# Last six steps of a seven-product down projection taken tile by tile, and the final LayerNorm of four tiles as two VectorE passes

## The chip, the core and the metric

The kernel runs on one core of one Trainium2 chip. The metric is device time in microseconds. Engines are named PE (TensorE matmul), PEld (TensorE weight load), DVE (VectorE), ACT (ScalarE), POOL (GpSimd) and SP (SyncE, which here only issues transfers).

## The reference, cut to what matters

The program is one inference step of a decoder layer for 1024 prompt tokens and 64 sample tokens, with 1024 model columns and an inner width of 2816. The part around the change is the second FFN and the last LayerNorm:

```
def layer_norm(x, g, b):
    xc = xf - mean(xf)
    return xc * rsqrt(mean(xc * xc) + LN_EPS) * g + b

def swiglu(x, wi, wo):
    g, u = split(x @ wi, 2)
    return (silu(g) * u) @ wo
...
x = layer_norm(ALPHA * x + 0.5 * swiglu(x, ffn_wi[0], ffn_wo[0]), ln_g[0], ln_b[0])
x = layer_norm(ALPHA * x + merged @ w_o, ln_g[1], ln_b[1])
x = layer_norm(ALPHA * x + 0.5 * swiglu(x, ffn_wi[1], ffn_wo[1]), ln_g[2], ln_b[2])
```

## The kernel before, in words

Every engine has its own program written out by hand, and engines wait for one another on counting semaphores. Nothing is scheduled by a planner in this part.

Both FFNs run the same code, `ffn(f)` with f = 0 and 1. The down product (`silu(g) * u` times `ffn_wo`) of the prompt is computed as seven block products, q = 0 to 6, instead of eight. Each product runs over KD = 11 blocks of the inner width, so there are STEPS = 77 steps t = 11q + k. One step brings a 128x512 block `h_raw` of activations and a 128x512 block of weights. Each f32 operand is split in two: ACT rounds it (`step_hi`: `h_hi`, `b_hi`, line L963 and L904), and DVE subtracts to get the rest (`step_lo`: `h_lo`, `b_lo`, L1397 and L1398, then `d_lo_ready`). PE then does four token tiles i = 0 to 3 of the step (`down_tile`), each with three matmuls of 512 columns (hi*hi, lo*hi, hi*lo; L2026 to L2028). Each tile i adds up in a PSUM bank of its own over the eleven steps. In the text "the lows of step t" are the two results of `step_lo` for step t.

Operands lie in three slots, t modulo 3. SP loads `h_raw` of step t once the lows of step t-3 are made; ACT writes slot t modulo 3 once PE has counted step t-3 as done (`step_done`). Between the lows of two steps DVE also does `step_extras`: it adds finished products into `y` and does the LayerNorm of tiles 0 to 3 and of the sample tile 8 (scale L1306, shift L1311, statistics L1550).

The last product, q = 6, is steps 66 to 76. PE takes steps 66 to 73 step by step. For the last three steps it waits for the lows of step 75, does steps 74 and 75 of tiles 0 and 1, waits for the lows of step 76, finishes tiles 0 and 1, and then does tile 2 and tile 3 whole. Tile i of this product becomes token tile 4+i of the output (columns 0 to 511; the other half was ready before).

After `ffn(1)` DVE adds each finished bank to `y` (L1285), takes the statistics of the half (L2006) and aggregates them (L2007). POOL makes the reciprocal root (`rstd`: add epsilon L730, power L731, minus mean times it L732). ACT normalises into two PSUM banks (L1238), DVE multiplies by the gain (L2011), and the shift by the bias is done on POOL for tiles 4 and 5 (L819, L821, L822) and on DVE for tiles 6 and 7 (L2014, L2016, L2017). SP stores tiles 0 to 3, 8, 4 and 5, ACT's queue stores tiles 6 and 7; tiles 5 and 7 go out in halves.

Of the kernel before, what the change touches and what calls it, by code (L numbers as in the profile page):

```python
# [277 lines left out]
def hybrid_layer(nc, w, c, o):  # L278
# [4 lines left out]
    with ExitStack() as ctx:  # L283
# [305 lines left out]
        def _(sp):  # L589
# [104 lines left out]
            store_y(8)  # L694
            store_y(4)
            wait_affine(sp, 2, 5)
            sp.dma_start(o["y_prompt"][0, 5 * P:6 * P, 0:512], y_half(5, 0)).then_inc(y_stored, 16)
            sp.wait_ge(ln_affine, affine_count(2, 5)[1] + 1)
            sp.dma_start(o["y_prompt"][0, 5 * P:6 * P, 512:D], y_half(5, 1)).then_inc(y_stored, 16)
            sp.wait_ge(y_stored, 16 * (NT + 2))  # L700
# [3 lines left out]
        def _(pool):  # L704
# [83 lines left out]
            def ffn(f):  # L788
# [26 lines left out]
                for t in range(4, 8):  # L815
                    rstd(k * NT + t + 1, t)
                if f:
                    pool.wait_ge(scaled_last, 1)
                    nc.gpsimd.tensor_tensor(y_tile(4), y_tile(4), ln_bd[:], ALU.add).then_inc(ln_affine, 1)  # L819
                    pool.wait_ge(scaled_last, 2)  # L820
                    nc.gpsimd.tensor_tensor(y_half(5, 0), y_half(5, 0), ln_bd[:, 0:512], ALU.add).then_inc(ln_affine, 1)  # L821
                    nc.gpsimd.tensor_tensor(y_half(5, 1), y_half(5, 1), ln_bd[:, 512:D], ALU.add).then_inc(ln_affine, 1)  # L822
# [1876 lines left out]
```

## Time and profile before

| | us |
|---|---|
| median of three runs | 2437.4 |
| lowest, highest | 2435.5, 2445.0 |
| span of the profiled execution (first to last instruction) | 2434.7 |
| DVE's last instruction ends | 2430.5 |
| PE's last matmul ends | 2421.7 |

The profiled execution has no device time of its own beside its span. The span lies 2.7 us under the median of the runs, and that difference is taken as what lies around it. All moments below are counted from the start of the span. In the profile of matmuls the start of one to the start of the next is the cost of one; the duration shown (0.39 us) includes a stretch that overlaps the next.

### The profile page before, as it was taken

The numbers are of one execution on the slowest core, as the hardware profiler recorded it, in microseconds if no ns is written. First come the engines' busy times: TensorE is split into PE (matmuls) and PEld (weight loads), VectorE is DVE, ScalarE is ACT, GpSimd is POOL, SyncE is SP. The second block draws the span as 40 slices with busy tenths as digits, with TensorE's granted clock in tenths as the row PEclk, the third lists the DMA queues.
The fourth block names the chain that finished last, engine by engine and source line by source line (L and its number), as shares of the span: only waits on it lengthen the run. The fifth ranks groups of instructions, "written<-read, shape, count | busy, mean of one in ns | idle before, by whom it ended". The sixth has DMA issues, their size and how long they took to land.

```text
span 2434.7 us, 31780 instructions
## 1 busy us (share of the span) xinstructions
PE 2395.3 (98%) x12613; PEld 2053.8 (84%) x12613; DVE 1660.1 (68%) x2305; ACT 910.8 (37%) x1325; POOL 205.3 (8%) x297
## 2 busy tenths in 40 slices
PE   8999999999999999999999999999999999999997
PEld 6888888888878898989999878888788888888786
DVE  6666565657787767666666867577866566665788
ACT  4222222243353336543347333373422222234344
POOL 3000000000021010000100111202300000000011
PEclk9999999999999999999999999999999999999999
DMA  4232222267444333243342445534222222327643
GB/s 144 87 125 82 89 89 95 83 218 232 131 140 142 110 111 111 96 127 90 114 126 87 140 141 169 169 96 148 74 97 81 96 100 91 104 96 225 200 147 129
DMA packets 225859, 300.08 MB, mean 123 GB/s; under 512 B 13424, under 2 KB 166304, under 8 KB 222880
## 3 DMA queue, kind: packets, MB, share of 16 engines
q1 hardware_dynamic: 211936, 240.43, 31.8%
q0 software_dynamic: 13056, 56.48, 6.3%
q8 instruction: 100, 1.64, 0.3%
q10 hardware_dynamic: 720, 1.15, 0.1%
q14 instruction: 47, 0.39, 0.0%
HBM read 243.81 MB, written 55.18 MB: 123 GB/s over the span
## 4 chain that ended last, share of the span: by engine, by line
PE 88%; DVE 6%; ACT 2%; DMA 2%; issue 1%; SPq 0%; POOL 0%; DVEq 0%; ACTq 0%
PE ps L2026 25%; PE ps L2027 25%; PE ps L2028 25%; PE ps L2123 2%; PE ps L2122 2%; PE ps L2202 1%; DVE xc_lo L1316 1%; PE ps L2203 1%; PE ps L2368 1%; DVE b_lo L1398 1%; DVE y L1285 1%; DVE w_lo L491 1%; PE ps L2503 1%; DMA raw<-in_w_in 1%; DVE h_lo L1397 1%
## 5 line engine op out<-in xcount | busy, mean ns | idle before, releaser
L2026 PE MATMUL ps<-xc_hi,u_hi 128*128 128x512 f32 x1232 | 482.7, 392 | 2.6 <-DVE u_lo L1357 1.5
L2027 PE MATMUL ps<-xc_lo,u_hi 128*128 128x512 f32 x1232 | 480.3, 390 | 0.0
L2028 PE MATMUL ps<-xc_hi,u_lo 128*128 128x512 f32 x1232 | 479.6, 389 | 0.0
L491 DVE TENSOR_TENSOR w_lo<-raw,w_hi 128x1024 fp32r<-128x1024 f32 x198 | 238.8, 1221 | 99.4 <-ACT w_hi L485 99.1
L2026 PEld LDWEIGHTS ps<-xc_hi,u_hi 128*128 128x128 f32 x1232 | 231.6, 188 | 49.2 <-DVE xc_lo L1316 1.7
L2028 PEld LDWEIGHTS ps<-xc_hi,u_lo 128*128 128x128 f32 x1232 | 231.2, 188 | 48.7
L2027 PEld LDWEIGHTS ps<-xc_lo,u_hi 128*128 128x128 f32 x1232 | 231.7, 188 | 44.7
L485 ACT ACTIVATE w_hi<-raw 128x1024 fp32r<-128x1024 f32 x198 | 205.5, 1054 | 161.4 <-PE ps L2028 95.6
L2026 PE MATMUL ps<-b_hi,h_hi 128*128 128x512 f32 x616 | 241.1, 391 | 1.7 <-DVE b_lo L1398 1.7
L2028 PE MATMUL ps<-b_hi,h_lo 128*128 128x512 f32 x616 | 239.8, 389 | 0.0
L2027 PE MATMUL ps<-b_lo,h_hi 128*128 128x512 f32 x616 | 239.7, 389 | 0.0
L2026 PE MATMUL ps<-w_hi,xg_hi 128*128 128x256 f32 (+1 forms) x640 | 219.2, 343 | 0.0
L2028 PE MATMUL ps<-w_hi,xg_lo 128*128 128x256 f32 (+1 forms) x640 | 215.1, 336 | 0.0
L2027 PE MATMUL ps<-w_lo,xg_hi 128*128 128x256 f32 (+1 forms) x640 | 215.0, 336 | 0.0
L963 ACT ACTIVATE h_hi<-h_raw 128x512 fp32r<-128x512 f32 x154 | 97.4, 632 | 271.2 <-PE ps L2028 175.5
L1357 DVE TENSOR_TENSOR u_lo<-wa,u_hi 128x1024 fp32r<-128x1024 f32 x88 | 108.8, 1236 | 107.3 <-ACT u_hi L904 107.3
L904 ACT ACTIVATE u_hi<-wa 128x1024 fp32r<-128x1024 f32 x88 | 93.0, 1057 | 203.6 <-PE ps L2123 109.9
L904 ACT ACTIVATE u_hi<-ws 128x1024 fp32r<-128x1024 f32 x66 | 70.0, 1060 | 241.9 <-PE ps L2028 148.3
L1397 DVE TENSOR_TENSOR h_lo<-h_raw,h_hi 128x512 fp32r<-128x512 f32 x154 | 106.0, 688 | 67.7 <-ACT b_hi L904 67.4
L2026 PEld LDWEIGHTS ps<-b_hi,h_hi 128*128 128x128 f32 x616 | 115.6, 188 | 30.1 <-issue 3.2
L2028 PEld LDWEIGHTS ps<-b_hi,h_lo 128*128 128x128 f32 x616 | 115.6, 188 | 24.4
L2027 PEld LDWEIGHTS ps<-b_lo,h_hi 128*128 128x128 f32 x616 | 115.6, 188 | 23.7
(330 smaller groups left out, 4572.9 us busy)
## 6 DMA issues: line engine op xcount, KB each, us to landing
raw<-in_w_in SPq DMA_DIRECT2D x90, 512.0 KB, 3.8
wa<-in_ffn_wi SPq DMA_DIRECT2D x88, 512.0 KB, 3.8
h_raw<-h_spill SPq DMA_DIRECT2D x154, 256.0 KB, 2.8
h_spill<-tm POOLq DMA_DIRECT2D x22, 1024.0 KB, 4.2
b_raw<-in_ffn_wo SPq DMA_DIRECT2D x66, 256.0 KB, 3.7
raw<-in_w_in SPq DMA_DIRECT2D x96, 128.0 KB, 2.5
raw<-in_w_in SPq DMA_DIRECT2D x48, 256.0 KB, 3.2
raw<-in_w_br_ret SPq DMA_DIRECT2D x24, 512.0 KB, 4.2
```

The source lines that it names most:

```text
L485: nc.scalar.activation(wslot(n, False), raw[:, s * D:(s + 1) * D], ACT.Copy).then_inc(hi_ready, 1)
L491: nc.vector.tensor_tensor(wslot(n, True), raw[:, s * D:(s + 1) * D], fr(wslot(n, False)), ALU.subtract).then_inc(lo_ready, 1)
L904: nc.scalar.activation(dst, src, ACT.Copy).then_inc(sem_, 1)
L963: nc.scalar.activation(h_hi[s][:], h_raw[s][:], ACT.Copy)
L1285: return nc.vector.scalar_tensor_tensor(out=out, in0=in0, scalar=scalar, in1=in1, op0=op0, op1=op1)
L1357: tt(u_lo[s][:], w_src[i][:], fr(u_hi[s][:]), ALU.subtract).then_inc(u_dve, 1)
L1397: tt(h_lo[s][:], h_raw[s][:], fr(h_hi[s][:]), ALU.subtract)
L2026: mm(out, a_hi, b_hi, start=first, stop=False)
L2027: mm(out, a_hi, b_lo, start=False, stop=False)
L2028: return mm(out, a_lo, b_hi, start=False, stop=last)
L2122: mm(out, lhs, u_hi[s][:, k * 2 * P:(k + 1) * 2 * P], start=first and k == 0, stop=False)
L2123: ins = mm(out, lhs, u_lo[s][:, k * 2 * P:(k + 1) * 2 * P], start=False, stop=last and k == 3)
```

## The change

For the second FFN alone, steps 71 to 73 write their split operands into three further slots (`end_...`), which lie where `t1` and the first column block of `t2` were, no longer read at that point. So steps 71 to 76 have six slots together. ACT no longer waits for PE before steps 71 to 73; for steps 74 to 76 it waits for step 68, 69, 70 to be done, as before in slot but without steps 71 to 73 between. `h_raw` keeps its three slots and its loads keep their waits. PE runs steps 0 to 70 as before and then takes steps 71 to 76 tile by tile: six steps of tile 0, where it waits in turn for the lows of each step, then six of tile 1, of tile 2 and of tile 3.

The first FFN has no further slots. Its last three steps are now also tile by tile from the first, with a wait for each step's lows, where before steps 74 and 75 of tiles 0 and 1 came ahead of the wait for step 76.

The final LayerNorm of tiles 4 to 7 is done by DVE alone but for the power: (y - mean) * gain in one pass and * rstd + bias in the next, both in `y`. DVE also adds epsilon, POOL does only the power, ACT does nothing but issue stores. DVE finishes a tile before it takes the next. Tile 7 is done in two halves. SP stores 8, 4 and 5 whole.

```
+        for j, tiles in enumerate((h_hi, h_lo, b_hi, b_lo)):
+            tiles += [at(f"end_{'hb'[j // 2]}{j % 2}_{i}", (149 + 2 * j + 8 * i) * K, 512, FR) for i in range(3)]
...
+        def slot_of_step(f, t):
+            return 3 + t - (STEPS - 6) if f and STEPS - 6 <= t < STEPS - 3 else t % 3
+        def steps_done_before(f, t):
+            return max(0, t - 5 if f and t >= STEPS - 3 else 0 if f and t >= STEPS - 6 else t - 2)
...
             def step_hi(f, t):
-                if t >= 3:
-                    act.wait_ge(step_done, STEPS * f + t - 2)
-                else:
+                if t < 3:
                     act.wait_ge(prod_done, product(f, UNITS - 1, 2))
+                elif steps_done_before(f, t):
+                    act.wait_ge(step_done, STEPS * f + steps_done_before(f, t))
...
-            for t in range(4, 8):
-                dve.wait_ge(ln_hat, hat_count(2, t))
-                dst = two_banks(LAST_BANK[t]) if t in DVE_AFFINE[2] else y_tile(t)
-                tt(dst, two_banks(LAST_BANK[t]), ln_gd[:], ALU.mult).then_inc(scaled_last, 1)
...
+                link(nc.vector.bn_aggr(mv[:, 2 * t:2 * t + 2], st6[:, 12 * t:12 * t + 12]))
+                nc.vector.tensor_scalar(ve[:, t:t + 1], mv[:, 2 * t + 1:2 * t + 2], LN_EPS, None, ALU.add).then_inc(ln_aggr, 1)
+                if t < 7:
+                    link(stt(y_tile(t), y_tile(t), mean, ln_gd[:], ALU.subtract, ALU.mult))
+                    dve.wait_ge(ln_rstd, hat_count(2, t))
+                    stt(y_tile(t), y_tile(t), rstd, ln_bd[:], ALU.mult, ALU.add).then_inc(ln_affine_v, 1)
+                    continue
+                for half in range(2):
+                    link(stt(yh, yh, mean, ln_gd[:, cols], ALU.subtract, ALU.mult))
+                    dve.wait_ge(ln_rstd, hat_count(2, t))
+                    stt(yh, yh, rstd, ln_bd[:, cols], ALU.mult, ALU.add).then_inc(ln_affine_v, 1)
...
-                last = STEPS - 3
-                pe.wait_ge(d_lo_ready, STEPS * f + last + 2)
-                for i in (0, 1):
-                    for t in (last, last + 1):
-                        down_tile(f, 6, i, t % KD, t % 3)
-                pe.wait_ge(d_lo_ready, STEPS * f + last + 3)
-                for i in (0, 1):
-                    down_tile(f, 6, i, KD - 1, (last + 2) % 3).then_inc(tile_done, 1)
+                for i in range(4):
+                    for t in range(first, STEPS):
+                        if i == 0:
+                            pe.wait_ge(d_lo_ready, STEPS * f + t + 1)
+                        ins = down_tile(f, 6, i, t % KD, slot_of_step(f, t))
```

(`first` is STEPS - 6 for the second FFN and STEPS - 3 for the first; `link` makes DVE wait for the instruction's own end.)

PE, end of the second FFN, before. Of each group of three matmuls the first stands here; `b_hi1,h_hi1` is step 73, `2` is step 74, `0` is step 75, then `1` step 76.

```order
L2026 MATMUL ps<-b_hi1,h_hi1 128x512 [waits d_lo_ready]
...
L2026 MATMUL ps<-b_hi1,h_hi1 128x512
...
L2026 MATMUL ps<-b_hi2,h_hi2 128x512 [waits d_lo_ready]
...
L2026 MATMUL ps<-b_hi0,h_hi0 128x512
...
L2026 MATMUL ps<-b_hi2,h_hi2 128x512
...
L2026 MATMUL ps<-b_hi0,h_hi0 128x512
...
L2026 MATMUL ps<-b_hi1,h_hi1 128x512 [waits d_lo_ready]
```

The same place in the change, from step 71 on (`end_b0_0` is the rounded weights of step 71, `end_b0_1` of 72, `end_b0_2` of 73):

```order
L2024 MATMUL ps<-end_b0_0,end_h0_0 128x512 [waits d_lo_ready]
...
L2024 MATMUL ps<-end_b0_1,end_h0_1 128x512 [waits d_lo_ready]
...
L2024 MATMUL ps<-end_b0_2,end_h0_2 128x512 [waits d_lo_ready]
...
L2024 MATMUL ps<-b_hi2,h_hi2 128x512 [waits d_lo_ready]
...
L2024 MATMUL ps<-b_hi0,h_hi0 128x512 [waits d_lo_ready]
...
L2024 MATMUL ps<-b_hi1,h_hi1 128x512 [waits d_lo_ready]
...
L2024 MATMUL ps<-end_b0_0,end_h0_0 128x512
```

Between two waits for lows there were twelve matmuls (four tiles) and are now three (one tile); 54 matmuls stand behind the last wait for tiles 1 to 3, where before there were 24 behind the wait for step 76.

DVE, the lows of steps 75 and 76 and what follows them, before:

```order
L1397 TENSOR_TENSOR h_lo0<-h_raw0,h_hi0 128x512 [waits d_hi_ready]
L1398 TENSOR_TENSOR b_lo0<-b21_t4,b_hi0 128x512
L1550 BN_STATS ln_stats<-y 128x6 [waits dve_step]
L1397 TENSOR_TENSOR h_lo1<-h_raw1,h_hi1 128x512 [waits d_hi_ready]
L1398 TENSOR_TENSOR b_lo1<-b21_t4,b_hi1 128x512
L1285 SCALAR_TENSOR_TENSOR y<-y,ps 128x512 [waits dve_step,tile_done]
L2006 BN_STATS ln_stats<-y 128x6 [waits tile_out]
L2007 BN_AGGR ln_mv<-ln_stats 128x2 [waits dve_step]
L1285 SCALAR_TENSOR_TENSOR y<-y,ps 128x512 [waits dve_step,tile_done]
```

The same place in the change:

```order
L1393 TENSOR_TENSOR h_lo0<-h_raw0,h_hi0 128x512 [waits d_hi_ready]
L1394 TENSOR_TENSOR b_lo0<-b21_t4,b_hi0 128x512
L1546 BN_STATS ln_stats<-y 128x6 [waits dve_step]
L1393 TENSOR_TENSOR h_lo1<-h_raw1,h_hi1 128x512 [waits d_hi_ready]
L1394 TENSOR_TENSOR b_lo1<-b21_t4,b_hi1 128x512
L1281 SCALAR_TENSOR_TENSOR y<-y,ps 128x512 [waits dve_step,tile_done]
L2002 BN_STATS ln_stats<-y 128x6 [waits tile_out]
L2003 BN_AGGR ln_mv<-ln_stats 128x2 [waits dve_step]
L2004 TENSOR_SCALAR ln_cols<-ln_mv 128x1 [waits dve_step]
L1281 SCALAR_TENSOR_TENSOR y<-y,ln_mv,ln_g_down 128x1024
L1281 SCALAR_TENSOR_TENSOR y<-y,ln_cols,ln_b_down 128x1024 [waits ln_rstd,dve_step]
L1281 SCALAR_TENSOR_TENSOR y<-y,ps 128x512 [waits dve_step,tile_done]
```

Up to the lows of step 76 nothing moved on DVE: the same instructions stand in the same order, those of steps 71 to 73 with other slots. Behind them each tile's two passes now stand ahead of the next tile's addition.

PE, end of the first FFN, before (`2` is step 74, `0` step 75, `1` step 76; the transposes of a tile of `y` stand in front):

```order
L2037 MATMUL ps<-ident,y 128x128 x7
L2026 MATMUL ps<-b_hi2,h_hi2 128x512 [waits d_lo_ready]
...
L2026 MATMUL ps<-b_hi0,h_hi0 128x512
...
L2026 MATMUL ps<-b_hi2,h_hi2 128x512
...
L2026 MATMUL ps<-b_hi0,h_hi0 128x512
...
L2026 MATMUL ps<-b_hi1,h_hi1 128x512 [waits d_lo_ready]
```

And in the change:

```order
L2035 MATMUL ps<-ident,y 128x128 x7
L2024 MATMUL ps<-b_hi2,h_hi2 128x512 [waits d_lo_ready]
...
L2024 MATMUL ps<-b_hi0,h_hi0 128x512 [waits d_lo_ready]
...
L2024 MATMUL ps<-b_hi1,h_hi1 128x512 [waits d_lo_ready]
...
L2024 MATMUL ps<-b_hi2,h_hi2 128x512
```

The wait for step 76 stood behind twelve matmuls and stands behind six.

## Rows read from the trace of the kernel before

**Rows 1.** The page: span, and the chain that ended last, by engine.

```profile
span 2434.7 us, 31780 instructions
...
PE 88%; DVE 6%; ACT 2%; DMA 2%; issue 1%; SPq 0%; POOL 0%; DVEq 0%; ACTq 0%
```

**Rows 2.** Timeline, PE, second FFN's end: start, duration, instruction, idle before it.

```profile
2403.51 0.39 PE L2026 MATMUL ps<-b_hi,h_hi 128*128 128x512 f32 x1
...
2413.23 0.50 PE L2026 MATMUL ps<-b_hi,h_hi 128*128 128x512 f32 x1 [1.40 <-DVE b_lo L1398]
...
2421.30 0.39 PE L2028 MATMUL ps<-b_hi,h_lo 128*128 128x512 f32 x1
```

**Rows 3.** Windows: length, busy (count) of PE, PEld, DVE, ACT, POOL; clock, DMA.

```profile
2392.50:2415.00 22.50, 21.10 (x94) 17.12 (x93) 22.47 (x35) 9.34 (x17) 0.00 (x0) 1.00 0.53 181
...
2422.00:2434.70 12.70, 0.00 (x0) 0.00 (x0) 8.32 (x10) 3.12 (x3) 6.62 (x8) 0.58 0.43 166
```

**Rows 4.** Timeline, DVE: the second low of steps 72 to 76.

```profile
2403.69 0.69 DVE L1398 TENSOR_TENSOR b_lo<-b_t,b_hi 128x512 fp32r<-128x512 f32 x1
...
2406.62 0.69 DVE L1398 TENSOR_TENSOR b_lo<-b_t,b_hi 128x512 fp32r<-128x512 f32 x1
...
2409.55 0.69 DVE L1398 TENSOR_TENSOR b_lo<-b_t,b_hi 128x512 fp32r<-128x512 f32 x1
...
2412.49 0.69 DVE L1398 TENSOR_TENSOR b_lo<-b_t,b_hi 128x512 fp32r<-128x512 f32 x1
...
2414.28 0.69 DVE L1398 TENSOR_TENSOR b_lo<-b_t,b_hi 128x512 fp32r<-128x512 f32 x1
```

**Rows 5.** Timeline, DVE, from the last tile's addition to the last instruction.

```profile
2421.72 0.69 DVE L1285 SCALAR_TENSOR_TENSOR y<-y,ps 128x512 f32<-128x512 f32 x1
2422.44 0.69 DVE L2006 BATCH_NORM_STATS2 ln_stats<-y 128x6 f32<-128x512 f32 x1
2423.17 0.21 DVE L2007 BATCH_NORM_AGGREGATE ln_mv<-ln_stats 128x2 f32<-128x12 f32 x1
...
2426.77 1.23 DVE L2014 TENSOR_TENSOR y<-ps,ln_b_down 128x1024 f32<-128x1024 f32 x1
2427.91 1.22 DVE L2011 TENSOR_TENSOR ps<-ps,ln_g_down 128x1024 f32<-128x1024 f32 x1
2429.17 0.69 DVE L2016 TENSOR_TENSOR y<-ps,ln_b_down 128x512 f32<-128x512 f32 x1
2429.78 0.68 DVE L2017 TENSOR_TENSOR y<-ps,ln_b_down 128x512 f32<-128x512 f32 x1
```

**Rows 6.** Timeline, POOL: the power for tile 7.

```profile
2423.77 0.56 POOL L731 TENSOR_TENSOR ln_cols<-ln_cols,neg_half 128x1 f32<-128x1 f32 x1
```

**Rows 7.** DMA issues: tile 4's store (2427.03) and the last store (2430.49), us to landing.

```profile
out_y_prompt<-y SPq DMA_DIRECT2D x1, 512.0 KB, 2.7
...
out_y_prompt<-y ACTq DMA_DIRECT2D x1, 256.0 KB, 3.8
```

**Rows 8.** Timeline, PE, first FFN: the seventh matmul behind the transposes.

```profile
726.68 0.40 PE L2026 MATMUL ps<-b_hi,h_hi 128*128 128x512 f32 x1
```

**Rows 9.** Timeline, DVE, first FFN: the second low of step 76.

```profile
726.47 0.68 DVE L1398 TENSOR_TENSOR b_lo<-b_t,b_hi 128x512 fp32r<-128x512 f32 x1
```

**Rows 10.** Windows, columns as in rows 3, where PE has little to do or its clock changes.

```profile
2421.00:2424.00 3.00, 0.69 (x4) 0.22 (x2) 2.86 (x6) 2.35 (x3) 1.85 (x7) 1.00 0.00 0
2424.00:2427.00 3.00, 0.00 (x0) 0.00 (x0) 2.97 (x4) 1.45 (x2) 2.90 (x4) 0.50 0.00 0
1725.00:1728.00 3.00, 1.21 (x8) 0.73 (x8) 3.00 (x5) 2.23 (x5) 2.92 (x2) 1.00 0.00 0
...
1645.00:1649.00 4.00, 4.00 (x16) 4.00 (x16) 2.21 (x5) 2.00 (x6) 0.00 (x0) 0.50 0.01 4
1649.00:1653.00 4.00, 4.00 (x29) 4.00 (x28) 0.00 (x0) 1.39 (x2) 0.00 (x0) 0.98 0.41 131
```

**Rows 11.** Timeline, PE: where dense 320-column matmuls begin before those windows.

```profile
1644.64 0.64 PE L2026 MATMUL ps<-xg_hi,w_hi 128*128 128x320 f32 x1
```

More of the change, by code:

```diff
@@ L693, in _ @@
             ffn(1)
[L694 to L700, printed above, removed]
+            for t in (8, 4, 5):
+                store_y(t)
+            sp.wait_ge(y_stored, 16 * (NT + 1))
         @block.gpsimd
@@ L814, in ffn @@
                     load_consts()
-                for t in range(4, 8):
[L816 to L822, printed above, removed]
+                if f == 0:
+                    for t in range(4, 8):
+                        rstd(t + 1, t)
+                else:
+                    for t in range(4, 8):
+                        pool.wait_ge(ln_aggr, 2 * NT + t + 2)
+                        nc.gpsimd.tensor_tensor(rs[:, t:t + 1], ve[:, t:t + 1], neg_half[:, 0:1], ALU.pow).then_inc(ln_rstd, 1)
                 if f == 0:
@@ L962, in step_hi @@
                     act.wait_ge(t3_ready, KD * f + k + 1)
-                nc.scalar.activation(h_hi[s][:], h_raw[s][:], ACT.Copy)
-                copy(b_hi[s][:], step_source(q, k, s), d_hi_ready)
+                nc.scalar.activation(h_hi[e][:], h_raw[s][:], ACT.Copy)
+                copy(b_hi[e][:], step_source(q, k, s), d_hi_ready)
             def first_sum(f):
@@ L1231, in _ @@
             ffn(1)
-            for t in range(4, 8):
-                act.wait_ge(ln_rstd, hat_count(2, t))
-                if t == 7:
-                    act.wait_ge(scaled_last, 1)
-                else:
-                    act.wait_ge(tile_out, 28 + (24, 26, 28)[t - 4])
-                nc.scalar.activation(two_banks(LAST_BANK[t]), y_tile(t), ACT.Identity, bias=nmr[:, t:t + 1],
-                                     scale=rs[:, t:t + 1]).then_inc(ln_hat, 1)
             wait_affine(act, 2, 6)
@@ L1384, in step_lo @@
             def step_lo(f, t):
-                s, q, k = t % 3, t // KD, t % KD
+                s, q, k, e = t % 3, t // KD, t % KD, slot_of_step(f, t)
                 n = KD * f + k
@@ L2006, in _ @@
                 link(nc.vector.bn_stats(st6[:, 12 * t:12 * t + 6], y_half(t, 0)))
-                nc.vector.bn_aggr(mv[:, 2 * t:2 * t + 2], st6[:, 12 * t:12 * t + 12]).then_inc(ln_aggr, 1)
-            for t in range(4, 8):
-                dve.wait_ge(ln_hat, hat_count(2, t))
-                dst = two_banks(LAST_BANK[t]) if t in DVE_AFFINE[2] else y_tile(t)
-                tt(dst, two_banks(LAST_BANK[t]), ln_gd[:], ALU.mult).then_inc(scaled_last, 1)
-                if t == 6:
-                    dve.wait_ge(scaled_last, 3)
-                    tt(y_tile(6), two_banks(LAST_BANK[6]), ln_bd[:], ALU.add).then_inc(ln_affine_v, 1)
-            dve.wait_ge(scaled_last, 4)
-            tt(y_half(7, 0), bank(LAST_BANK[7]), ln_bd[:, 0:512], ALU.add).then_inc(ln_affine_v, 1)
-            tt(y_half(7, 1), bank(LAST_BANK[7] + 1), ln_bd[:, 512:D], ALU.add).then_inc(ln_affine_v, 1)
+                link(nc.vector.bn_aggr(mv[:, 2 * t:2 * t + 2], st6[:, 12 * t:12 * t + 12]))
+                nc.vector.tensor_scalar(ve[:, t:t + 1], mv[:, 2 * t + 1:2 * t + 2], LN_EPS, None, ALU.add).then_inc(ln_aggr, 1)
+                mean, rstd = mv[:, 2 * t:2 * t + 1], rs[:, t:t + 1]
+                if t < 7:
[4 more added lines that the diff above has]
+                for half in range(2):
+                    cols, yh = slice(half * 512, (half + 1) * 512), y_half(t, half)
+                    link(stt(yh, yh, mean, ln_gd[:, cols], ALU.subtract, ALU.mult))
+                    dve.wait_ge(ln_rstd, hat_count(2, t))
+                    stt(yh, yh, rstd, ln_bd[:, cols], ALU.mult, ALU.add).then_inc(ln_affine_v, 1)
         @block.tensor
@@ L2217, in ffn @@
                 fold_sample(f, UNITS - 1)
-                for t in range(STEPS - 3):
+                first = STEPS - (6 if f else 3)
+                for t in range(first):
                     q, k, sl = t // KD, t % KD, t % 3
```

19 lines of the change are left out of this document (8 added, 11 removed).

## The prediction

> **What bounds the kernel now.** I read the page first: the span is 2434.7 us and PE holds 88% of the chain that ended last [rows 1]. So a microsecond added to or taken from PE's work in the down product is nearly a microsecond of time, and only the stretch after PE's last matmul belongs to other engines. Then the timeline of PE at the end of the second FFN [rows 2]: matmuls follow each other without a gap from 2403.51 to the end of step 73, PE then waits 1.40 us for DVE's lows of step 75, restarts at 2413.23, and its last matmul starts at 2421.30 and ends at 2421.69. From 2413.23 to 2421.30 there are 35 intervals; less the 0.11 us by which the first is longer, one matmul costs 0.227 us, a tile of a step 0.68, a step 2.73.
>
> The third view is the one that decides this case, the windows [rows 3]. From 2392.5 to 2415.0 DVE is busy for 22.47 of 22.50 us. So the pace at which the lows are made in steps 68 to 76 is DVE's own: it waits neither for ACT, nor for a load, nor for PE. The lows of steps 72 to 76 are finished at 2404.38, 2407.31, 2410.24, 2413.18 and 2414.97 [rows 4].
>
> After PE's end, DVE works from 2421.72 without a pause to 2430.46 [rows 5], the last store is issued at 2430.49, lands after 3.8 us [rows 7], and the span ends 4.2 us after that issue. From 2421.69 to the end are thus 13.0 us, with no matmul in them [rows 3].
>
> **The six slots.** The edit lets ACT round steps 71 to 73 earlier, by not waiting for PE. What was waiting for ACT there? Only DVE, and DVE was never idle. The order of DVE's instructions up to the lows of step 76 is unchanged (the change section), so the lows come at the same moments as before: worth 0. What hides ACT is DVE's backlog; if it were gone, a load still stands behind the lows of step t-3. SP's queue has the same transfers in the same order. I take the moments of [rows 4] as they are.
>
> **PE tile by tile, second FFN.** PE used to spend 2.73 us between two waits for lows; for tile 0 it now spends 0.68. Step 71 of tile 0 can start at 2403.51 [rows 2]. Then each step of tile 0 waits for its lows, plus the 0.05 us between 2413.18 and 2413.23 [rows 2, 4]: step 72 at 2404.43, 73 at 2407.36, 74 at 2410.29, 75 at 2413.23 and 76 at 2415.02. Between them PE does little. What is queued behind these waits is all of tiles 1, 2 and 3, ready in operands for steps 71 to 75 but standing behind the wait for step 76. From 2415.02 there are 3 + 54 = 57 matmuls: 56 x 0.227 + 0.11 + 0.39 = 13.2, so PE ends at 2428.25 instead of 2421.69: **+6.6 us**. Tile 0 is finished at 2415.97, tile 1 at 2420.07, tile 2 at 2424.16, tile 3 at 2428.25.
>
> **The two-pass LayerNorm.** Per tile on DVE, counted from the start of its addition [rows 5]: statistics at 0.72, aggregate at 1.45. Then the added epsilon at 1.68 (aggregate's 0.21 plus 0.02 for the wait on itself). No row here shows a 128x1 operation of DVE in this place; the nearest is the 0.21 us aggregate, and I bound its cost by 0 and 0.23 and take 0.10, since it isn't waited for by the next pass. First pass at 1.78. Second pass 1.25 later (1.23 and a wait of 0.02), at 3.03. POOL's power has started by then at about 1.98 and takes 0.56 [rows 6], so rstd is there at 2.6: 0.4 us of cover; without it each tile would wait. The next tile's addition comes 1.14 after, the interval between the full-width operations at 2426.77 and 2427.91 [rows 5]. Sum 4.17 us per tile, against PE's 54 / 3 x 0.227 = 4.09. So DVE, from 2416.00, takes tile 5 at 2420.17, tile 6 at 2424.34, tile 7 at 2428.51. Tile 7 in halves: first pass at 1.78, second pass at 2.60 (it waits for POOL here), first pass of the other half 0.61 later, the interval between the last two rows of [rows 5], its second pass at 3.93, end at 4.62. The last store is issued 4.65 after 2428.51: 2433.16. Before it was 2430.49: **+2.7 us**. So a tail of 8.8 us from PE's end to the last issue has become 4.9, of the 6.6 lost on PE 3.9 come back.
>
> A rule to weigh here: the Trainium skill (VectorE: DVE Perf Modes, section "The DRAIN you can't avoid") says that the next vector operation cannot start before the pipe is empty and that a semaphore between two costs nothing extra. The rows do not agree with the second half: with a wait the next operation starts 0.72 us after a 512-wide one, without 0.61 [rows 5]. By the page the two unwaited hand-overs in each tile would cost some 0.2 us more per tile, about +0.5 us on the sum; the measured intervals decide.
>
> **The stores.** Before, 2 MB went out at once after 2427, and the last store took 3.8 us; tile 4's, which went alone, took 2.7 for twice the bytes [rows 7]. Now tiles 4 to 6 leave one at a time, 4 us apart. A lone 256 KB is bounded by 2.0 (my estimate, 2.7 less half the transfer of 512 KB) and 3.8; nearest is the lone one, I take 2.4: **-1.4 us**. ACT's and SP's issues are hidden behind DVE's passes.
>
> **First FFN.** Its wait for step 76 now stands behind six matmuls, not twelve. The seventh matmul started at 726.68 [rows 8]; the lows of step 76 are there at 727.15 [rows 9]. PE stops 0.5 us and pays 0.1 for the restart. Behind it PE runs on without slack for a long stretch, and it has 88% of the chain: **+0.5 us** (0 to 0.6). The tiles' earlier ends bring nothing, DVE adds them up later. ACT, DVE and POOL do there what they did.
>
> **PE's clock.** From 2405.3 to 2415.0 PE would have three bursts of 0.96 us, 2.9 in 9.7 us: 0.9 in each 3 us. In the trace the granted clock stood at full (2.4 GHz) over a window with 1.21 us of work in 3 (1725 to 1728), and it fell to half (1.2 GHz) at 2424 after one with 0.69 in 3 [rows 10]. The new stretch lies between, repeats itself over ten microseconds, and I expect the clock to fall in it. The bursts themselves can double without harm, since PE is waiting anyway; the harm comes after 2415.02. At the one earlier fall dense matmuls ran from 1644.64 [rows 11] at half clock until just past 1649: 16 in 4 us against 29 at full [rows 10], so 4.4 us did the work of about 2.3. Cost **+2.1 us** on everything behind. DVE's small excess over PE is then no longer added: tile 4 begins at 2416.6 and is finished long before tile 5's bank at 2422.2, and tile 7 begins at 2430.54. Last issue 2435.19, against 2433.16: +2.0.
>
> **Sum.** Last issue +2.7, stores -1.4, first FFN +0.5: +1.8 us with the clock up; +3.8 us with the clock down for 4.4 us. Against the profiled execution: 2434.7 + 3.8 = 2438.5 of span. With the 2.7 us by which the median of the runs lies above the span: **2441.2 us**. The measurement of this kernel tells nothing from no change within 0.5%, some 12 us, so this is a forecast of no change, on its slow side.
>
> **The rivals.**
> 1. The same stall, but PE's clock stays up (the 1725 window speaks for it, as do single waits of 1.4 us at full clock [rows 2]; the length of the thin stretch speaks against): +1.8, 2439.2 us.
> 2. The change does what its shape suggests, tiles spread out with no stall. Then PE ends at about 2421.3 as without its 1.40 us wait plus restarts, the last issue is 4.9 after, the store lands 1.4 sooner: 2426.2 against 2430.49, -4.3 - 1.4 + 0.5 = -5.2, 2432.2 us. It needs the lows of step 76 at 2403.51 + 5 x 0.68 = 2406.9, where the rows have them at 2414.97 and DVE has 0.03 us of idle time to give. Almost excluded; a part of it (DVE faster with POOL and ACT quieter) is thinkable.
> 3. Slower by more than 0.5%: the clock falls between 2405 and 2415 and does not come back before PE is done. A 512-column matmul then costs about 0.43 (4 us / 15 intervals x 512 / 320), 57 of them 24.3 us instead of 13.2: +11.1 + 1.8, 2450.3 us. It decides only if the half clock lasts for the whole of the 24 us; in the trace it lasted about 4.4 us of dense work.
>
> **How the numbers follow.** Clock falls and recovers 0.55; rival 1 0.30; rival 2 or a part of it 0.05; rival 3 0.04; something unseen 0.06. The range: below, rival 1 with the lone store at 2.0 and nothing lost in the first FFN is 2438.3, and the three runs spread some 2 us under their median; above, 2441.2 with the half clock a further 2 us, the epsilon at its upper bound (0.4) and the page's hand-overs is 2444. I give 2436.3 to 2444.5. Faster by over 0.5% (under 2425) 0.01, slower by over 0.5% (over 2449.6) 0.04, the rest 0.95.
>
> **What would show it.** Right: PE waits for DVE's `b_lo` four times for about 2 us and once for 1 us between 2405 and 2415, its last matmul ends at 2428 to 2431, the lows of step 76 still end near 2415, DVE's last instruction ends near 2433 to 2435, the last landing takes under 3 us, and the clock reads 0.50 in a window between 2407 and 2420. Wrong: lows of step 76 well before 2414, DVE idle among the steps, second passes that wait for POOL in every tile, or a difference that sits before 2400.

## The result, and the profile after

The changed kernel's time is 2445.06 us, the median of 20 runs (2441.34 to 2450.41). The kernel before, run 20 times beside it on the same chip, had 2440.43 us (2435.47 to 2445.0). The ratio is 1.0019, with the interval 1.0014 to 1.0025: 4.6 us longer (3.4 to 6.1). That is clear of the noise, and within the 0.5% that the prediction counts as no change, on its slow side. The forecast was 2441.2 us, which against its base of 2437.4 is a ratio of 1.0016: that ratio lies within the interval, while the time lies 3.9 us above the forecast and 0.6 us above the range. Of all the executions compared in this document one, of the kernel *eager end* below, fell in a slow state (4008.5 us) and is left out of its ratio.

The page of the changed kernel: span, busy time by engine, and the chain that ended last.

```profile
span 2442.9 us, 31769 instructions
...
PE 2402.1 (98%) x12613; PEld 2055.6 (84%) x12613; DVE 1664.4 (68%) x2312; ACT 905.9 (37%) x1321; POOL 202.4 (8%) x286
...
PE 88%; DVE 6%; DMA 2%; ACT 2%; issue 1%; SPq 0%; POOL 0%; DVEq 0%; ACTq 0%; POOLq 0%
```

The span is 8.2 us longer than in [rows 1]. Step 71's first matmul starts at 2407.09, and at 2403.51 in [rows 2], so 3.6 us of the difference lie ahead of any instruction of the changed end. All but 0.1 us of them, left from the first FFN, have nothing to do with the change (last section). All that follows is counted from the start of step 71's first matmul; by that count the end comes after 35.8 us, and after 31.2 before: +4.6 us, which is also what the medians show. That is one profiled execution of each kernel; the medians are over 20.

The timeline of PE there (start, duration, instruction, idle before it), which answers to [rows 2]:

```profile
2407.09 0.39 PE L2024 MATMUL ps<-end_b,end_h 128*128 128x512 f32 x1
...
2408.02 0.50 PE L2024 MATMUL ps<-end_b,end_h 128*128 128x512 f32 x1
...
2410.95 0.50 PE L2024 MATMUL ps<-end_b,end_h 128*128 128x512 f32 x1 [1.97 <-DVE end_b L1394]
...
2413.88 0.80 PE L2024 MATMUL ps<-b_hi,h_hi 128*128 128x512 f32 x1 [1.97 <-DVE b_lo L1394]
...
2416.82 0.80 PE L2024 MATMUL ps<-b_hi,h_hi 128*128 128x512 f32 x1 [1.28 <-DVE b_lo L1394]
...
2418.61 0.80 PE L2024 MATMUL ps<-b_hi,h_hi 128*128 128x512 f32 x1 [0.15 <-DVE b_lo L1394]
...
2433.13 0.39 PE L2026 MATMUL ps<-b_hi,h_lo 128*128 128x512 f32 x1
```

PE waits for the lows of steps 73 to 76. The idle times shrink from 1.97 to 1.28 us because a burst of three matmuls takes 1.65 us in the later ones (2413.88 to 2415.53) where it took 0.97: the first matmul after a wait takes 0.80 us where it took 0.50. The last one shrinks to 0.15 us because, besides, the lows of step 76 follow those of step 75 after 1.80 us and not after 2.93. The windows, columns as in [rows 3], show why the bursts are longer, in the column of the granted clock:

```profile
2411.00:2414.00 3.00, 1.03 (x4) 0.56 (x4) 3.00 (x5) 0.93 (x3) 0.00 (x0) 0.67 0.63 210
2414.00:2417.00 3.00, 1.72 (x4) 0.90 (x5) 3.00 (x5) 0.98 (x2) 0.00 (x0) 0.50 1.04 425
2417.00:2420.00 3.00, 2.85 (x6) 1.81 (x7) 1.56 (x3) 0.00 (x0) 0.00 (x0) 0.50 0.61 239
2420.00:2423.00 3.00, 3.00 (x10) 2.31 (x9) 2.60 (x5) 0.00 (x0) 0.76 (x1) 0.63 0.00 0
2423.00:2426.00 3.00, 3.00 (x15) 2.49 (x14) 2.24 (x3) 0.00 (x0) 0.75 (x1) 1.00 0.00 0
```

It stands at half (1.2 GHz) from 2412.0 to 2422.2. The first column of busy time is PE's; beside it DVE is busy for 3.00 of 3.00 us until 2417.

The timeline of DVE and of POOL's power, from the last low to the last pass; it answers to [rows 4 to 6]:

```profile
2417.88 0.68 DVE L1394 TENSOR_TENSOR b_lo<-b_t,b_hi 128x512 fp32r<-128x512 f32 x1
2420.30 0.69 DVE L1281 SCALAR_TENSOR_TENSOR y<-y,ps 128x512 f32<-128x512 f32 x1 [1.74 <-PE ps L2026]
...
2430.15 0.68 DVE L1281 SCALAR_TENSOR_TENSOR y<-y,ps 128x512 f32<-128x512 f32 x1
2430.86 0.69 DVE L2002 BATCH_NORM_STATS2 ln_stats<-y 128x6 f32<-128x512 f32 x1
2431.59 0.21 DVE L2003 BATCH_NORM_AGGREGATE ln_mv<-ln_stats 128x2 f32<-128x12 f32 x1
2431.84 0.15 DVE L2004 TENSOR_SCALAR ln_cols<-ln_mv 128x1 f32<-128x1 f32 x1
2431.91 1.28 DVE L1281 SCALAR_TENSOR_TENSOR y<-y,ln_mv,ln_g_down 128x1024 f32<-128x1024 f32 x1
2433.69 1.28 DVE L1281 SCALAR_TENSOR_TENSOR y<-y,ln_cols,ln_b_down 128x1024 f32<-128x1024 f32 x1 [0.51 <-POOL ln_cols L826]
2434.90 0.68 DVE L1281 SCALAR_TENSOR_TENSOR y<-y,ps 128x512 f32<-128x512 f32 x1
...
2439.36 0.75 DVE L1281 SCALAR_TENSOR_TENSOR y<-y,ln_cols,ln_b_down 128x512 f32<-128x512 f32 x1
```

```profile
2432.07 1.52 POOL L826 TENSOR_TENSOR ln_cols<-ln_cols,neg_half 128x1 f32<-128x1 f32 x1 [3.23 <-DVE ln_cols L2004]
```

The last low is finished 11.47 us into the stretch, and 11.46 before. Then from one addition to the next a tile takes DVE 4.75 us (2430.15 to 2434.90), with 0.51 us of waiting for POOL's power in it. That power takes 1.52 us, against 0.56 in [rows 6]. The last store is issued at 2440.14 and the span ends 2.8 us later, where it was 4.2 us. DVE's chain hangs on PE only at its first tile and, by 0.24 us, at its second (the release of `y<-y,ps` at 2425.39); tiles 6 and 7 find their banks ready.

### The profile page after: what moved, and what is told of

It is laid out like the page before. It is cut to its first block, busy times and chain, and to the rows that moved or that the text cites. A ratio compares the mean times of both kernels' runs of the same rounds, so it can differ in the third digit from the quotient of the medians.

```text
span 2442.9 us, 31769 instructions
## 1 busy us (share of the span) xinstructions
PE 2402.1 (98%) x12613; PEld 2055.6 (84%) x12613; DVE 1664.4 (68%) x2312; ACT 905.9 (37%) x1321; POOL 202.4 (8%) x286
## 4 chain that ended last, share of the span: by engine, by line
PE 88%; DVE 6%; DMA 2%; ACT 2%; issue 1%; SPq 0%; POOL 0%; DVEq 0%; ACTq 0%; POOLq 0%
PE ps L2024 25%; PE ps L2025 25%; PE ps L2026 25%; PE ps L2121 2%; PE ps L2120 2%; DMA b_raw<-in_ffn_wo 1%; DVE xc_lo L1312 1%; DVE b_lo L1394 1%; PE ps L2200 1%; PE ps L2201 1%; PE ps L2363 1%; DVE y L1281 1%; PE ps L2498 1%; DVE h_lo L1393 1%; PE ps L2475 1%
## 5 line engine op out<-in xcount | busy, mean ns | idle before, releaser
L2024 PEld LDWEIGHTS ps<-w_hi,xg_hi 128*128 128x128 f32 x640 | 121.8, 190 | 14.3 <-issue 1.2
```

Source lines behind the costliest of these rows:

```text
L2024: mm(out, a_hi, b_hi, start=first, stop=False)
```

## The experiments

All are compared with the kernel before, run beside them. The table gives us from the start of step 71's first matmul, in the one profiled execution of each.

| kernel | PE's end | last low | additions of tiles 4, 5, 6, 7 | last issue | end | ratio of times [interval] |
|---|---|---|---|---|---|---|
| before | 18.18 | 11.46 | 13.45 15.03 16.56 18.21 | 26.98 | 31.19 | 1 |
| changed | 26.43 | 11.47 | 13.21 18.30 23.06 27.81 | 33.05 | 35.81 | 1.0019 [1.0014, 1.0025] |
| order alone | 25.77 | 11.45 | 13.20 17.65 21.73 25.81 | 34.58 | 38.78 | 1.0034 [1.0021, 1.0047] |
| LayerNorm alone | 18.17 | 11.46 | 13.45 18.21 22.96 27.70 | 32.95 | 35.76 | 1.0014 [1.0005, 1.0023] |
| three steps | 18.62 | 11.47 | 12.52 17.28 22.03 26.77 | 32.02 | 34.75 | 1.0015 [1.0006, 1.0024] |
| power first | 26.68 | 11.46 | 13.20 18.56 23.59 28.62 | 34.14 | 36.90 | 1.0027 [1.0018, 1.0036] |
| PE kept busy | 24.78 | 11.46 | 12.53 17.30 22.05 26.79 | 32.04 | 34.76 | 1.0020 [1.0010, 1.0030] |
| late extras | 23.47 | 7.94 | 13.75 18.50 23.25 28.00 | 33.24 | 35.99 | 1.0018 [1.0009, 1.0027] |
| pipelined | 18.65 | 11.48 | 12.54 14.61 18.89 23.17 | 30.45 | 33.24 | 1.0015 [1.0006, 1.0024] |
| eager end | 16.81 | 11.45 | 12.76 14.34 15.87 17.40 | 26.13 | 30.30 | 0.9992 [0.9983, 1.0001] |
| eager and spread | 16.81 | 11.46 | 12.77 14.35 15.88 18.50 | 26.29 | 30.05 | 0.9988 [0.9979, 0.9997] |
| eager, spread, late | 16.70 | 10.91 | 11.96 13.53 15.06 17.68 | 25.49 | 29.18 | 0.9996 [0.9987, 1.0006] |

The theory after the result: PE's stall is real, but DVE's two-pass chain of 4.75 us a tile sets the end, and part of those 4.75 us is POOL's power, which is held up (0.51 us of waiting). The rival: PE's stall sets the end and DVE only follows, so that taking the stall away gives most of the loss back.

**Order alone.** The changed order of steps and the six slots, with the LayerNorm of before (the two LayerNorm parts of the diff left out).

> Only the six slots and PE's tile-by-tile order, with the LayerNorm tail of before (ACT normalises, POOL shifts two tiles). Measured by the stretch from the first matmul of step 71 to the end of the span: 31.2 us before, 35.8 us with the whole change. Theory (PE stands behind lows that come at DVE's pace, and 57 matmuls follow the last wait; the new LayerNorm gives part back): PE's last matmul ends 26.4 us after step 71 starts, as with the whole change (18.2 before), the old tail of 13.0 us follows it whole, so 39.4 us, 8.2 more than before; with 0.6 us of the first FFN some 0.36% slower. Rival (the loss is made by the two-pass LayerNorm and POOL's slow power, and PE's order is harmless because tiles 4 to 6 finish early): under 33 us, within 0.1% of before.

Measured: +7.6 us in the stretch. Here PE does set the pace: DVE waits 2.42 us for PE's bank in each tile (2429.45 to 2433.53 is 4.08 us, PE's tile), and behind the last addition comes the whole old tail. The end is 0.6 us sooner than expected, since PE is: its half clock began earlier in the stretch (3.5 us in) and was over 13.8 us in, in the changed kernel 15.2. The timeline of DVE, order alone:

```profile
2429.45 0.69 DVE L1295 SCALAR_TENSOR_TENSOR y<-y,ps 128x512 f32<-128x512 f32 x1 [2.42 <-PE ps L2038]
...
2433.53 0.69 DVE L1295 SCALAR_TENSOR_TENSOR y<-y,ps 128x512 f32<-128x512 f32 x1 [2.42 <-PE ps L2038]
...
2439.72 1.22 DVE L2021 TENSOR_TENSOR ps<-ps,ln_g_down 128x1024 f32<-128x1024 f32 x1
```

**LayerNorm alone.** The two passes, with the order of before (the slots, `step_hi`, `step_lo` and PE's loop as they were, in both FFNs).

> Only the two-pass LayerNorm of tiles 4 to 7, with PE's order and the three slots of before. Step 71 to the end: 31.2 us before. Theory that the PE order alone is the loss and the new tail gives back about 4 us: 28 us or less, faster by 0.1%. Rival (DVE is the bound of the tail: 4.75 us a tile instead of the 4.17 of the prediction, four tiles one behind the other from tile 4's end at 13.5 us): tile 7 begins at 27.7, the last store is issued at 32.9, the end at 35.7 us, 4.5 more than before and the same as the whole change, 0.18% slower. POOL's power lasts 1.5 us in both.

Measured: +4.6 us, as much as the whole change, with PE's end at 18.17, where it always was. The parts do not add (7.6 and 4.6 against 4.6): the end is the later of two chains, and DVE's is the later one. The timelines of DVE and POOL, LayerNorm alone:

```profile
2429.11 1.27 DVE L1271 SCALAR_TENSOR_TENSOR y<-y,ln_mv,ln_g_down 128x1024 f32<-128x1024 f32 x1
2430.90 1.28 DVE L1271 SCALAR_TENSOR_TENSOR y<-y,ln_cols,ln_b_down 128x1024 f32<-128x1024 f32 x1 [0.51 <-POOL ln_cols L816]
```

```profile
2429.28 1.52 POOL L816 TENSOR_TENSOR ln_cols<-ln_cols,neg_half 128x1 f32<-128x1 f32 x1 [3.24 <-DVE ln_cols L1994]
```

The power runs from 2429.28 to 2430.80, the pass beside it from 2429.11 to 2430.38. It ends 0.42 us after the pass, and that end is what the next pass waits for.

**Three steps.** The changed kernel, tile by tile over the last three steps and not six, from three slots.

```diff
-                first = STEPS - (6 if f else 3)
+                first = STEPS - 3
```

(`slot_of_step` gives `t % 3` and `steps_done_before` gives `t - 2`.)

> The whole change, but tile by tile over the last three steps of the second FFN as in the first, with three slots. PE waits for lows only at steps 75 and 76, its thin stretch is short, so the granted clock should stay at full. Theory (wait order): PE's last matmul ends 18.6 us after step 71 starts instead of 26.4. If DVE's tail of 4.75 us a tile is the bound: tile 4 begins at 12.5, tile 7 at 26.8, the end comes at 34.8 us, only 1.0 under the whole change although PE ends 7.8 us sooner. If PE's end is what counts: 18.6 + 1.4 + 5.2 + 2.8 = 28 us.

Measured: PE ends 7.8 us earlier than in the changed kernel, at 18.62, and the end of the span comes only 1.1 us earlier. So of PE's stall and its half clock together 1.1 us reach the end. The rival falls. The clock stayed at full.

**Power first.** DVE waits for rstd before the first pass, so that nothing on DVE runs beside the power.

```diff
+                dve.wait_ge(ln_rstd, hat_count(2, t))
                 if t < 7:
                     link(stt(y_tile(t), y_tile(t), mean, ln_gd[:], ALU.subtract, ALU.mult))
-                    dve.wait_ge(ln_rstd, hat_count(2, t))
```

> The whole change, but DVE waits for rstd before the first pass of each tile instead of before the second, so that POOL's power runs while DVE does nothing. Theory (POOL's power is held up while DVE reads two SBUF tensors in its first pass, 1.51 us against 0.56 before): the power takes 0.56 us again, the first pass starts 0.8 us later, the second has no wait, a tile takes 5.0 us instead of 4.75, 1 us more in all. Rival (the power is slow because it now follows DVE's added epsilon, or because POOL was idle long): it still takes 1.5 us, a tile takes 5.9 us, 4.5 us more in all.

The timeline of POOL, power first:

```profile
2423.99 0.55 POOL L826 TENSOR_TENSOR ln_cols<-ln_cols,neg_half 128x1 f32<-128x1 f32 x1 [4.81 <-DVE ln_cols L2004]
2429.01 0.55 POOL L826 TENSOR_TENSOR ln_cols<-ln_cols,neg_half 128x1 f32<-128x1 f32 x1 [4.48 <-DVE ln_cols L2004]
```

The same instruction takes 0.55 us when DVE stands still and 1.51 beside a pass. A tile then takes 5.03 us (18.56 to 23.59), since the whole power is now waited for: slower than 4.75, and the end comes 1.1 us later. This shows that the pass beside it makes the 1.5 us, and not the added epsilon or POOL's idle time. Hiding the power behind a pass of its own tile saves 0.28 us of its 0.55 and no more.

What it is in the pass that holds the power can be read from the kernel before. The timelines of POOL and of DVE there, in another stage and after tile 4's addition:

```profile
888.14 1.39 POOL L845 TENSOR_TENSOR gn_cols<-gn_cols,neg_half 128x1 f32<-128x1 f32 x1
...
2419.01 0.56 POOL L731 TENSOR_TENSOR ln_cols<-ln_cols,neg_half 128x1 f32<-128x1 f32 x1
```

```profile
887.88 1.22 DVE L491 TENSOR_TENSOR w_lo<-raw,w_hi 128x1024 fp32r<-128x1024 f32 x1
...
2418.54 0.64 DVE L1285 SCALAR_TENSOR_TENSOR y<-y,ps 128x512 f32<-128x512 f32 x1
```

At 888.14 POOL does the same operation, and DVE subtracts two tensors that both lie in SBUF, with another instruction than that of the passes and without a per-partition scalar. The power takes 1.39 us and ends 0.43 us after the subtraction. At 2419.01 it takes 0.56 us beside DVE's addition of a bank in PSUM to `y`, which is the instruction of the passes but with one tensor in SBUF. So what goes with the hold-up is the second tensor in SBUF. The 1.39 us stood in the trace of the kernel before; the prediction took its 0.56 from the one place of [rows 6].

**PE kept busy.** In the waits of tile 0, PE does extra matmuls into a bank that nothing reads any more, enough to leave it hardly any idle time. One more wait of PE, ahead of step 71, makes sure that the bank has been read.

```diff
+FILL = (8, 9, 9, 4)
...
+                        if i == 0 and f and t == first:
+                            pe.wait_ge(y8_out, 4)
+                        if i == 0 and f and first + 2 <= t:
+                            e = slot_of_step(f, first)
+                            for _ in range(FILL[t - first - 2]):
+                                mm(bank(7), h_hi[e][:, 0:P], b_hi[e][:], start=True, stop=True)
```

> The whole change with PE's waits for the lows of steps 73 to 76 in tile 0 filled by 8, 9, 9 and 4 extra matmuls of 512 columns into a PSUM bank that nothing reads any more. Theory (the thin stretch of PE pulls the granted clock to half): the clock stays at full from step 71 to PE's end, which comes 24.7 us after step 71 starts instead of 26.4; tile 4 begins at 12.5 instead of 13.2. DVE's four tiles of 4.75 us follow, so tile 7 begins at 26.7 and the stretch from step 71 to the end is 34.7 us instead of 35.8. If PE's end set the end, the gain would be 1.7 us; if the clock falls for another reason, nothing changes.

The windows of this kernel over the same stretch (it starts at 2402.44):

```profile
2408.00:2411.00 3.00, 3.00 (x14) 2.23 (x14) 3.00 (x5) 1.15 (x2) 0.00 (x0) 1.00 1.02 412
2411.00:2414.00 3.00, 3.00 (x14) 1.99 (x12) 2.90 (x5) 0.00 (x0) 0.00 (x0) 1.00 1.02 406
2414.00:2417.00 3.00, 3.00 (x14) 2.47 (x14) 1.93 (x5) 0.00 (x0) 0.09 (x1) 1.00 0.07 26
```

The clock stays at 1.00 until PE is done. PE's end is at 24.78, where the forecast without a clock had 24.74 (2428.25 less 2403.51). The half clock thus cost 1.65 us on PE's end and 1.05 us on the end of the span (35.81 against 34.76). Of that, 0.68 is tile 4's later start and 0.32 the later bank of tile 5. The times do not resolve it: 1.05 us are 0.04%, and the ratio is 1.0020, with an interval that holds the changed kernel's 1.0019. How much the half clock costs also depends on when it begins: with the same program of PE its end is at 25.77 in *order alone* and at 26.68 in *power first*, 1.0 and 1.9 us above 24.78.

**Late extras.** DVE's other work between the lows of steps 72 to 76 is moved behind the steps.

```diff
+                if f and q == 6 and r >= 6:
+                    return
```

(and after the steps: `affine_shift(2, 3)`, four half statistics, `affine_scale` and `affine_shift` of tile 8)

> The whole change, with DVE's other work of steps 72 to 76 (shift of tile 3, scale and shift of tile 8, four half statistics, together 5.8 us) moved behind the lows of step 76. Theory (DVE's backlog sets when the lows come): the lows of step 76 come 7.6 us after step 71 starts instead of 11.5, held then by the loads, and PE ends at 20.8 instead of 26.4. The moved work stands ahead of tile 4's addition, so DVE's tail begins where it did, at 13.4, tile 7 at 27.7, and the end stays at 35.7 us: PE's stall costs the whole change nothing beside DVE's tail. Rival (PE's stall is what the 4.6 us are made of): the end comes 4 to 5 us sooner, at 31 us.

Measured: the last low comes at 7.94 instead of 11.47, and the end 0.2 us later than in the changed kernel. The moved work stands ahead of tile 4's addition, and DVE has the same sum to do. PE's end was missed: 23.47, expected at 20.8. The granted clock fell to half here too, at 2413.1 in a wait of 1.44 us, and stayed there for 6.8 us. With DVE faster among the steps, the next wait shows up, for ACT. The timelines of DVE and of ACT, late extras:

```profile
2411.82 0.69 DVE L1393 TENSOR_TENSOR h_lo<-h_raw,h_hi 128x512 fp32r<-128x512 f32 x1 [1.11 <-ACT b_hi L908]
```

```profile
2410.64 0.63 ACT L967 ACTIVATE h_hi<-h_raw 128x512 fp32r<-128x512 f32 x1 [1.25 <-DMA h_raw<-h_spill]
```

ACT in turn waits for the load, which by the code waits for the slot behind the lows of three steps before. That is the backlog that hides ACT, as the prediction had it.

**Pipelined.** Three steps as above, and the passes of a tile come one tile later, so that the power has a whole addition and its statistics to finish in.

```diff
+            add_and_stats(4)
+            for t in (5, 6, 7):
+                add_and_stats(t)
+                two_passes(t - 1)
+            two_passes(7)
```

> three_steps (the changed LayerNorm, three slots) with DVE's order changed: it adds and measures the next tile before it does the two passes of a tile, so that POOL's power for tiles 4 to 6 runs while DVE waits for PE or adds from PSUM. three_steps needed 34.75 us from step 71 to the end, with 0.5 us of waiting for POOL in each tile. Theory (POOL's power is held up while DVE reads two SBUF tensors, and this lengthens each tile): the power takes 0.56 us for tiles 4 to 6 again, the second passes start without a wait, tile 7's addition comes at 23.1, the last issue at 30.4, the stretch is 33.1 us. That is still 2 us above before: four tiles with both passes on DVE are longer than the old split over ACT, DVE and POOL. If the hold-up costs nothing on the chain, 34.7 us again.

Measured: no second pass waits, and a tile takes 4.28 us. Tile 4's power, beside no pass, took 0.55 us. For the others the expectation was wrong: those of tiles 5 to 7 started 0.17 us behind the start of the other tile's first pass and took 1.52 us again, but nobody waits for them yet. The timelines of POOL and DVE, pipelined:

```profile
2431.68 1.52 POOL L826 TENSOR_TENSOR ln_cols<-ln_cols,neg_half 128x1 f32<-128x1 f32 x1 [2.75 <-DVE ln_cols L2003]
```

```profile
2431.51 1.28 DVE L1281 SCALAR_TENSOR_TENSOR y<-y,ln_mv,ln_g_down 128x1024 f32<-128x1024 f32 x1
2432.82 1.28 DVE L1281 SCALAR_TENSOR_TENSOR y<-y,ln_cols,ln_b_down 128x1024 f32<-128x1024 f32 x1
```

The stretch is 1.5 us shorter than with three steps (33.24 against 34.75), and still 2.05 us longer than before. What is left is the two passes: one tile is 4.28 us on DVE alone, and ACT, which did the normalizing before, has no pass left to do. From the changed kernel back to the one before, the 4.6 us are thus 1.1 for PE's stall with its half clock (three steps), 1.5 for the waits for the power (pipelined) and 2.0 for both passes on DVE.

**The other way: leave LayerNorm, mend PE's wait.** In the kernel before, PE waits for the lows of step 75 with matmuls of step 74 undone, and after PE's end only the LayerNorm of the last tiles is left. Three kernels start from the kernel before. *Eager end* gives tiles 0 and 1 each step as its lows come:

```diff
+                if f:
+                    for n in range(3):
+                        pe.wait_ge(d_lo_ready, STEPS * f + last + n + 1)
+                        for i in (0, 1):
+                            ins = down_tile(f, 6, i, (last + n) % KD, (last + n) % 3)
...
+                        if n == 1:
+                            down_tile(f, 6, 2, last % KD, last % 3)
```

> The kernel before with one edit: in the last three steps of the second FFN PE waits for the lows of each step apart, and does tile 2 of step 74 while it waits for step 76. Nothing of the changed LayerNorm or slots. Theory: the 1.40 us wait of before goes, PE ends 16.8 us after step 71 starts instead of 18.2, tile 4 begins at 12.75 instead of 13.45, DVE's tail is then without a gap and the stretch is 30.4 us instead of 31.2: 0.8 us faster, 0.03%. If PE's end set the tail it would be 1.4 us.

*Eager and spread* also scales tile 4 ahead of tile 7's addition, and POOL shifts it ahead of tile 7's power, so that its store leaves earlier:

```diff
+                if t == 7:
+                    dve.wait_ge(ln_hat, hat_count(2, 4))
+                    tt(y_tile(4), two_banks(LAST_BANK[4]), ln_gd[:], ALU.mult).then_inc(scaled_last, 1)
```

> As greedy_end, and DVE multiplies tile 4 by the gain before it adds tile 7, POOL shifts tile 4 before it makes tile 7's rstd, so that tile 4's store leaves some 2.4 us sooner and the last stores find fewer bytes ahead. Expected: last issue as in greedy_end, 26.2 us after step 71 starts, last landing 3.2 us instead of 3.8, the stretch 29.8 us, 1.4 us under before. If POOL's shift of 2.35 us makes rstd of tile 7 late, DVE waits for ACT before tile 7's scale and the gain is gone.

*Eager, spread, late* also moves the shift of tile 8 from between the lows of steps 74 and 75 to behind those of step 76, and PE takes no matmuls of tile 2 between the steps:

```diff
-                if q == 6 and r == 8 and f:
-                    affine_shift(2 * f, NT - 1)
...
             ffn(1)
+            affine_shift(2, NT - 1)
```

> As greedy_spread, and the shift of tile 8 stands behind the lows of step 76 on DVE instead of ahead of those of step 75; PE does tiles 0 and 1 of each of the last three steps without tile 2 between. Theory (the lows come at DVE's pace, and DVE was idle for 1.3 us behind them): the lows of step 76 come at 10.7 instead of 11.46, the shift fills DVE's idle time, tile 4 begins at 11.9 instead of 12.77 us, and the stretch from step 71 to the end is 29.2 us instead of 30.05, 2.0 under before. If the lows are held by the loads or by ACT instead, tile 4 begins at 12.7 and nothing is gained.

Measured: the stretch is 30.3, 30.05 and 29.18 us, against 31.19. The timeline of PE's last matmul, eager and spread (it starts at 2407.75), shows that PE is done 16.81 us in, not 18.18. Of these 1.4 us 0.9 are left at the end (eager end); the earlier store adds 0.25.

```profile
2424.17 0.39 PE L2032 MATMUL ps<-b_hi,h_lo 128*128 128x512 f32 x1
```

Of these only *eager and spread* is told apart from the kernel before by its times: 0.12% faster, 0.03 to 0.21%. That is the weakest of findings: one interval of three just clear of 1, and a gain in the stretch of 1.1 us, which is 0.05%. What is safe is that all three stay ahead of the changed kernel, whose interval begins at 1.0014. The third has the shortest stretch, 2.0 us less than before, but its runs gave 0.9996 and an interval that holds 1, so what it adds is seen in one trace and not in the times. There DVE is first seen waiting for ACT among the steps (0.46 us ahead of step 76's lows), the next wait on this path.

## Why the prediction was right in its sign and wrong in its time

**What bounds the kernel, and the lows.** As predicted. DVE is busy throughout the steps, the lows of step 76 come at 11.47 us (11.46 before), and ACT's earlier rounding gives nothing.

**PE tile by tile.** The mechanism is as predicted: PE waits for `b_lo` and everything else stands behind the last wait. With the clock held up its end is at 24.78 us against 24.74. The sign named, four waits of about 2 us and one of 1, did not come (two of 1.97, then 1.28 and 0.15); the prediction's own moments give three and one, and the half clock shortens the later ones.

**The clock.** It fell in the thin stretch, as taken. It stayed at half from 2412.0 to 2422.2, of which 3.7 us lie behind the last low (2418.56), not 4.4. Its cost on PE's end was 1.65 us (predicted 2.1) and on the last issue 1.0 (predicted 2.0), since DVE's chain is slower than PE's tiles and takes up the rest.

**The two-pass LayerNorm: a term that was mis-sized.** "POOL's power has started by then at about 1.98 and takes 0.56 [rows 6]" and "0.4 us of cover". It takes 1.51, and the cover becomes a wait of 0.51 us. With the passes' 0.05 us more (1.28 for 1.23), a tile takes 4.75 us, not 4.17. With the clock up (PE kept busy) the last issue comes at 32.04, and by the sum at 29.65 (2433.16 less 2403.51): 2.4 us too little, of which four tiles by 0.58 are 2.3. The prediction named its own sign of being wrong, "second passes that wait for POOL in every tile", and that is what all four tiles do. The row of [rows 6] was read in a place where no pass with two tensors in SBUF ran beside it. The Trainium skill (GPSIMD Engine Reference, section "Specifications") says that GpSimd's interface to SBUF is shared with VectorE and contended when a vector instruction has two SBUF inputs. By that rule the power would be held here, since both tensors that a pass reads are in SBUF, and the trace agrees. The page gives no size; the traces do: 0.55 us unheld, 1.51 held, and 1.39 at 888.14 in the kernel before.

**"Of the 6.6 lost on PE 3.9 come back": a wrong attribution.** What remains isn't PE's loss. With PE's loss taken away (three steps, LayerNorm alone) the end is still 3.6 and 4.6 us late. PE's stall is hidden behind DVE's chain, all but 1.1 us of it.

**The stores.** 2.76 us from the last issue to the end, taken as 2.8. This was luck: the last store landed after 2.0 us, not 2.4, and from its landing to the end of the span it took 0.8 us, where before it was 0.4.

**First FFN.** The stop is there: PE waits 0.39 us. The timeline of PE, changed kernel:

```profile
727.26 0.50 PE L2024 MATMUL ps<-b_hi,h_hi 128*128 128x512 f32 x1 [0.39 <-DVE b_lo L1394]
```

But the +0.5 us does not reach the end whole. The kernel before had a pause at about 754, which the changed one hasn't; the timeline of PE, kernel before:

```profile
754.59 0.87 PE L2332 MATMUL ps<-ident,qk 128*128 128x128 f32 x6 [0.30 <-DVE qk L1736]
```

Against the kernel before, PE's matmuls in the changed kernel start 0.06 us later at 720, 0.70 later at 733 and 0.19 later at 769, so "PE runs on without slack for a long stretch" was wrong after 27 us. In each of the seven kernels with this edit the shift rises by some 0.6 us and falls by 0.5 between these places: 0.1 us is left.

**The sum.** In the stretch +3.3 us were predicted and +4.6 measured. The errors are +2.4 (power and passes) and -1.0 (clock). The first FFN adds -0.4 (0.1 for 0.5). Over the whole kernel +3.8 us were predicted, and the medians differ by 4.6: +0.8. That the forecast of the difference came so near is in part luck, since a term that was 2.4 us too small met two that were 1.4 too large.

**The base: the step that put the time outside.** "With the 2.7 us by which the median of the runs lies above the span." That median was of three runs, 2437.4, which themselves reached from 2435.47 to 2445.0; the median of 20 runs is 2440.43, 3.0 us higher. A time lies only 2.0 us above its own span (2444.94 and 2442.9 for the profiled run of the changed kernel). The rest of what was put on top stood for the difference between one run and the median, and was too small by 3.0. The range took two microseconds for the spread of the runs below and nothing above, where one of the three stood 7.6 us above their median. Of the 3.9 us by which the time missed, 3.0 are the base and 0.8 the sum.

## What to carry to other kernels

Where two chains run side by side to the end, cost each of them to its own last store, and take the later one. A saving or a loss in the other is worth only what sticks out (here 1.1 of PE's 7.8 us). The duration of a small operation on POOL holds only for the neighbour it was measured beside: before it is called hidden behind an operation of DVE, look at where that operation's inputs lie, and look up every place of the trace where the small operation runs (here 0.56, 0.86 and 1.39 us in one trace). Where the difference in question is smaller than the spread of the runs, forecast it against the base with the whole spread on both sides, not against a median of three.
